# Half of an output projection moved, in bursts of four matmuls, into the attention ahead of it

## The reference, cut to what matters

```python
def dilated_mixer(x, norm_gain, w_q, q_gain, w_o, k_sh, v_sh, cos, sin):
    ...
    for g, (window, dilation) in enumerate(DIL_GROUPS):      # three groups
        o_g, lse_g = dilated_group_attention(q[:, :, g], k_sh[:, :, g], v_sh[:, :, g], window, dilation)
    ...
    wts = jax.nn.softmax(jnp.stack(lses, axis=0), axis=0)
    o = jnp.sum(wts[..., None] * jnp.stack(outs, axis=0), axis=0)
    return o.astype(x.dtype).reshape(B, S, H * D) @ w_o

def squared_relu_mlp(x, gain, w_up, w_down):
    h = rms_norm_2(x, gain)
    return jnp.square(jax.nn.relu(h @ w_up)) @ w_down

x = x + dilated_mixer(x, ...)
x = x + squared_relu_mlp(x, m_norm[layer], m_w_up[layer], m_w_down[layer])
```

## Time and profile before

| | |
|---|---|
| median of 3 runs | 2930.29 us |
| the profiled execution's own time | 2930.43 us |
| its span in the profile | 2928.6 us |
| PE busy | 2835.1 us (97%) |
| DVE busy | 1732.2 us (59%) |
| ACT busy | 1224.2 us (42%) |
| POOL busy | 1080.7 us (37%) |

### The profile page before, as it was taken

How to read it: one execution, slowest core, us unless ns; L and a number is a source line. 1 busy time by engine, 2 the same in 40 slices (tenths; PEclk the granted TensorE clock), 3 DMA queues, 4 the chain that set the end, 5 groups by cost and what they waited for, 6 DMA issues and landing times.

```text
span 2928.6 us, 39102 instructions
## 1 busy us (share of the span) xinstructions
PE 2835.1 (97%) x13391; PEld 2317.9 (79%) x13402; DVE 1732.2 (59%) x2111; ACT 1224.2 (42%) x2067; POOL 1080.7 (37%) x498
## 2 busy tenths in 40 slices
PE   6999999999899999999889999999999999999999
PEld 5767788887777888888667888888888888888887
DVE  7487776775566544658566333557566766644333
ACT  3574432223564422244454222356566665522221
POOL 1312344443213444444324444444412342244443
PEclk9999999999899999999999999999999999999999
DMA  6255263643102333332003333333301321133332
GB/s 218 87 166 194 80 207 100 202 132 100 37 29 79 93 97 96 93 94 89 29 23 95 97 96 93 94 95 89 94 22 52 95 87 30 51 94 94 100 94 93
DMA packets 366140, 278.96 MB, mean 95 GB/s; under 512 B 13618, under 2 KB 321203, under 8 KB 366003
## 3 DMA queue, kind: packets, MB, share of 16 engines
q1 hardware_dynamic: 364752, 276.83, 31.0%
q10 hardware_dynamic: 1251, 0.33, 0.0%
HBM read 275.03 MB, written 2.10 MB: 95 GB/s over the span
## 4 chain that ended last, share of the span: by engine, by line
PE 65%; issue 3%; DVE 2%; ACT 2%; POOL 1%; DMA 0%; POOLq 0%; DVEq 0%; ACTq 0%; SPq 0%
PE banks L1186 13%; PE banks L1181 12%; PE banks L1190 12%; PE banks L1050 6%; PE banks L1056 6%; PE banks L1053 6%; PE banks L1455 2%; PE banks L1023 1%; PE banks L1395 1%; PE banks L1183 1%; PE banks L1384 0%; PE banks L1091 0%; POOL w_lo L895 0%; PE banks L1428 0%; PE banks L1430 0%
## 5 line engine op out<-in xcount | busy, mean ns | idle before, releaser
L895 POOL TENSOR_TENSOR w_lo<-w_raw,w_hi 128x1024 fp32r<-128x1024 f32 (+2 forms) x431 | 1030.2, 2390 | 1692.7 <-ACT w_hi L1703 1691.6
L1703 ACT ACTIVATE w_hi<-w_raw 128x1024 fp32r<-128x1024 f32 (+2 forms) x432 | 447.2, 1035 | 1117.4 <-PE banks L1190 783.9
L1050 PE MATMUL banks<-w_hi,h_hi 128*128 128x512 f32 x960 | 386.6, 403 | 0.7 <-ACT h_hi L1884 0.7
L1056 PE MATMUL banks<-w_lo,h_hi 128*128 128x512 f32 x960 | 377.0, 393 | 0.7 <-POOL w_lo L895 0.7
L1053 PE MATMUL banks<-w_hi,h_lo 128*128 128x512 f32 x960 | 376.0, 392 | 0.7 <-DVE h_lo L601 0.7
L1181 PE MATMUL banks<-h_hi,w_hi 128*128 128x512 f32 x1280 | 339.7, 393 | 8.2 <-ACT h_hi L1884 6.3
L1186 PE MATMUL banks<-h_lo,w_hi 128*128 128x512 f32 x1280 | 321.1, 391 | 2.5 <-DVE h_lo L601 2.4
L1181 PEld LDWEIGHTS banks<-h_hi,w_hi 128*128 128x128 f32 x1280 | 241.4, 189 | 65.4 <-issue 10.6
L1186 PEld LDWEIGHTS banks<-h_lo,w_hi 128*128 128x128 f32 x1280 | 240.3, 188 | 57.8 <-DVE h_lo L601 8.6
L1190 PE MATMUL banks<-h_hi,w_lo 128*128 128x512 f32 x1152 | 284.5, 389 | 0.0
L1190 PEld LDWEIGHTS banks<-h_hi,w_lo 128*128 128x128 f32 x1152 | 216.3, 188 | 44.8
(11 more groups left out here) (373 smaller groups left out, 4252.0 us busy)
## 6 DMA issues: line engine op xcount, KB each, us to landing
Z<-in_ada_w SPq DMA_DIRECT2D x64, 512.0 KB, 5.5
w_raw<-in_m_w_up SPq DMA_DIRECT2D x64, 512.0 KB, 4.0
w_raw<-in_m_w_down SPq DMA_DIRECT2D x64, 512.0 KB, 3.7
w_raw<-in_kv_w SPq DMA_DIRECT2D x48, 512.0 KB, 3.7
w_raw<-in_ffn_w_gate SPq DMA_DIRECT2D x44, 512.0 KB, 3.7
w_raw<-in_ffn_w_up SPq DMA_DIRECT2D x44, 512.0 KB, 3.7
tmp<-in_ada_w SPq DMA_DIRECT2D x32, 512.0 KB, 4.6
w_raw<-in_ffn_w_down SPq DMA_DIRECT2D x32, 512.0 KB, 3.9
```

Of the source, the lines that this page charges most:

```text
L895: pool.tensor_tensor(wlo[j][:, 0:n], raw[j][:, 0:n], whi[j][:, 0:n], ALU.subtract).then_inc(s_wlo, 1)
L1050: pe.matmul(t, hh, wh, start=k == 0, stop=False)
L1056: mm = pe.matmul(t, hh, wl, start=False, stop=k == DC - 1)
L1703: act.activation(whi[par][:, 0:kc * P], raw[par][:, 0:kc * P], ACT.Copy).then_inc(s_whi, 1)
```

## The change

The last projection is cut in two by its inner dimension. The first four chunks (heads of pairs 0 to 3) become a stage of their own, `second_half`: eight units of 12 matmuls, which PE runs within the attention's second half, in bursts of four, in parts q = 0, 1, 2 and 4, 5, 6 of each pair (in the first pair 4, 5, 6 only); the last unit runs behind the last values. All eight accumulate in bank 7. Their weights take half of buffer 0 each (`fill_tile`), since the attention uses buffer 1. For that the maxima's groups of these pairs go round three banks, 0, 1, 2, and the wait for `diagonal` stands at group 0. ACT, POOL and DVE get the copies, splits and additions of the eight units at fixed places of their order. The stage behind the attention keeps the other four chunks, 12 matmuls a unit. ACT now copies its first unit's weights behind `inverse` of the last pair, and its second unit's behind `y_high`; before, the first stood ahead of the attention and the second in the last pair.

```diff
@@ -460,7 +460,10 @@
                 panel(a["kv_w_2"], 3 * D + g * D + half * S, 24 + 4 * g, perm=g, fold="kv_norm")
             steps.append(("dil", 4 * half))
             panels[-1].first_pair = 4 * half
-        gemm_stage("down", 8, DC, a["b_w_o_2"][0], "y", gate=None)
+        wo = a["b_w_o_2"][0]
+        second_half = Stage("down", DC, FILL, [cols_of(wo, 0, FILL, j * P, 2 * P) for j in range(2)], "y")
+        gemm_stage("down", DC, DC - FILL, wo, "y", k0=FILL * P, gate=None)
+        steps[-1][1].first_chunk = FILL
         mlp(1)
         steps.append(("bar", None))
 
@@ -476,7 +479,7 @@
             if kind == "diff":
                 st = next(st for k, st in steps[n:] if k == "gemm")
                 st.early = st.after_diff = True
-        stages = [st for k, st in steps if k in ("gemm", "diff")]
+        stages = [second_half if k == "dil" else st for k, st in steps if k in ("gemm", "diff") or (k == "dil" and st == NB)]
         for s0, s1 in zip(stages, stages[1:] + [None]):
             s0.next_kc, s0.next = s1.kc if s1 else None, s1
             assert s0.base % 2 == 0
@@ -681,9 +684,17 @@
         dil_inverse = TMP[:, 12 * VW + 2 * S:12 * VW + 3 * S]
         dil_spread = TMP[:, 12 * VW + 3 * S:12 * VW + 3 * S + 2 * P]
 
+        def dil_ring(p):
+
+            return 4 if p < NB else 3
+
         def dil_bank(p, f):
 
-            return bank[(6, 7)[f % 2] if p % NB == 0 else DIL_BANKS[f % 4]]
+            return bank[(6, 7)[f % 2] if p % NB == 0 else DIL_BANKS[f % dil_ring(p)]]
+
+        def fill_tile(t, l):
+
+            return t[0][:, l % 2 * FILL * P:(l % 2 + 1) * FILL * P]
 
         def dil_turned(p):
             return dil_bank(p, 6)[:, P:P + 2 * NB]
@@ -911,6 +922,11 @@
                 zero([dil_rows(t, 0, par, HALF[1 - par]) for par in range(2) for t in (whi[1], wlo[1])]
                      + [t[:, first:first + 8, :] for first in (8, 16, 0) for t in by_quarter])
                 pool.wait_ge(dl["scores"], past(8 * base + 4))
+                if base:
+                    for l in range(DC):
+                        u = second_half.base + l
+                        pool.wait_ge(s_whi, past(u + 1))
+                        pool.tensor_tensor(fill_tile(wlo, l), raw[l % 2][:, 0:FILL * P], fill_tile(whi, l), ALU.subtract).then_inc(s_wlo, 1)
 
             def zero(todo):
                 for rows in todo:
@@ -1077,8 +1093,8 @@
 
                 half, m, first = f % 2, dil_bank(p, f), p % NB == 0
                 g = f // 2 + 1 if f < 4 else 0
-                pe.wait_ge(dl["reduced"], past(8 * p + f - (1 if first else 3)))
-                if f == 2:
+                pe.wait_ge(dl["reduced"], past(8 * p + f - (1 if first else dil_ring(p) - 1)))
+                if f == (2 if first or p < NB else 0):
                     pe.wait_ge(dl["diagonal"], past(3 * p))
                 if f in (0, 2, 4):
                     pe.wait_ge(dl["q_high"], past(3 * p + (2 if first and g == 0 else BY_GROUP[g])))
@@ -1455,6 +1471,25 @@
                             mm = pe.matmul(o, dil_vals[:, at:at + P], dil_probs[q % 2][:, own:own + width], start=g == 0 and c == 0, stop=g == 2 and c == NB - 1, skip_group_check=True)
                     mm.then_inc(e["values_added"], 1)
 
+                def fill(l, first=0, n=3 * FILL):
+
+                    par, u = l % 2, second_half.base + l
+                    if first == 0:
+                        if l:
+                            pe.wait_ge(evac[1 - par], past((u - 1) // 2 + 1))
+                        else:
+                            pe.wait_ge(e["reduced"], past(8 * base + 8))
+                            pe.wait_ge(e["output_high"], past(FILL))
+                            pe.wait_ge(e["output"], past(2 * FILL))
+                        pe.wait_ge(s_whi, past(u + 1))
+                        pe.wait_ge(s_wlo, past(u + 1))
+                    for i in range(first, first + n):
+                        k, part = divmod(i, 3)
+                        w, y = ((whi, yhi), (wlo, yhi), (whi, ylo))[part]
+                        mm = pe.matmul(bank[7], fill_tile(w, l)[:, k * P:(k + 1) * P], ch(y, k), start=i == 0, stop=i == 3 * FILL - 1)
+                    if i == 3 * FILL - 1:
+                        mm.then_inc(gemm, 1)
+
                 last = next(st for st in panels if st.first_pair == base)
                 zero_rows_in(2)
                 for p in range(base, base + NB):
@@ -1474,7 +1509,11 @@
                             zero_rows_in(2)
                         for f in ahead.get(q, []):
                             dil_fill(p + 1, f)
+                        if base and q % 4 < 3 and (q >= 4 or p > base):
+                            fill(2 * (p - base) + q // 4 - 1, 4 * (q % 4), 4)
                     values(p, 7)
+                if base:
+                    fill(DC - 1)
 
             def diff(st):
                 e = df
@@ -2078,6 +2117,13 @@
 
                     act.activation(ch(hhi, c), ch(xT, c), ACT.Copy).then_inc(n_hi, 1)
 
+                def fill_high(l):
+
+                    u = second_half.base + l
+                    act.wait_ge(w_raw[u % 2], 16 * (u // 2 + 1))
+                    act.wait_ge(gemm, past(u - 1))
+                    act.activation(fill_tile(whi, l), raw[u % 2][:, 0:FILL * P], ACT.Copy).then_inc(s_whi, 1)
+
                 last = next(st for st in panels if st.first_pair == base)
                 following = last.next
                 act.wait_ge(gemm, past(last.base + last.n))
@@ -2090,6 +2136,8 @@
                     probs(p, 0)
                     if old is not None:
                         take(p - 1, 1)
+                    if base:
+                        fill_high(max(2 * (p - base), 1))
                     if new is not None:
                         for par in range(2):
                             q_high(new, 1, par)
@@ -2122,8 +2170,10 @@
                     if new is not None:
                         q_high(new, 0, 0)
                         q_high(new, 0, 1)
-                    else:
+                    elif base == 0:
                         high(following.kc, 1, following.base + 1, following.base // 2, following, 1)
+                    if base and p > base:
+                        fill_high(2 * (p - base) + 1)
                     probs(p, 5)
                     if old is not None:
                         y_high(p - 1)
@@ -2140,10 +2190,14 @@
                 take(p, 0)
                 take(p, 1)
                 inverse(p)
+                if base:
+                    high(following.next.kc, 0, following.next.base, following.next.base // 2)
                 if base == 0:
                     h_again(6)
                     h_again(7)
                 y_high(p)
+                if base:
+                    high(following.next.kc, 1, following.next.base + 1, following.next.base // 2)
 
             def diff(st):
                 e = df
@@ -2790,16 +2844,28 @@
                     negate(p)
                     class_spread(p)
 
+                def take_fill(l):
+
+                    if not base:
+                        return
+                    u = second_half.base + l
+                    dve.wait_ge(gemm, past(u + 1))
+                    dve.tensor_tensor(ch(xT, l), bank[7], ch(xT, l), ALU.add).then_inc(evac[u % 2], 1)
+
                 def prepare(new, old):
 
                     if new is not None:
                         k_low(new, 1)
                     if old is not None:
                         output(old - 1)
+                        if new is None:
+                            take_fill(5)
                     if new is not None:
                         reduce(new, 0)
                         k_low(new, 2)
                         reduce(new, 1)
+                        if old is not None:
+                            take_fill(2 * (old - base) - 1)
                         reduce(new, 2)
                         reduce(new, 3)
                         rows_spread(new)
@@ -2830,6 +2896,7 @@
                         class_spread(p)
                     q_low(p, 2)
                     prepare(p + 1 if p < base + NB - 1 else None, p if p > base else None)
+                    take_fill(2 * (p - base))
                 p, h_lows = base + NB - 1, iter(DIL_LOWS)
                 again = next(n for n in norm_list if n.raw and not n.fresh)
 
@@ -2843,6 +2910,7 @@
                     low_again(6)
                     low_again(8)
                 output(p)
+                take_fill(DC - 1)
                 sub_low(p)
                 if base == 0:
                     dve.wait_ge(e["output"], past(2 * p + 2))
```

## The result

The changed kernel took 2934.74 us (median of 12 runs, 2930.84 to 2939.85), the kernel before 2930.13 us in the same rounds (12 runs, 2927.48 to 2933.70): ratio 1.0016, 95% interval 1.0008 to 1.0023. By the ratio that is 4.7 us slower (2.3 to 6.7). The forecast was 6.6 us slower, 2936.9 us in a range of 2933.0 to 2940.5. The growth of 0.16% is inside what I had called "no change" (0.2%), to which I had given less (0.39) than to a time beyond it (0.57).

A forecast was written before the change was run, and what follows sets the result against it. PE, busy 97% of the span, was taken as the bound, with little waiting to fill. The terms +1.0 - 1.5 + 2.45 + 3.86 + 0.8 gave +6.6 us on 2930.3: 2936.9 us, 8-in-10 range 2933 to 2940.5.

The forecast's parts named there:

- Part 1: Pairs 4 to 7 and projection: 96 matmuls leave (-21.8 us), return as bursts (19.05) and a last unit (2.72); net zero.
- 6: The seven other projection units behind the attention: 84 matmuls in 19.05 us without a gap, saving counted in Part 1.
- Part 2: Entry of bursts in the pairs: 12 of 21 cost 0.085 us each, +1.0 us (bounds 0 and 1.8).
- Part 3: Pairs 5 and 6: the two PE waits of 0.76 us for ACT go, -1.5 us (bounds -1.5 and 0).
- Part 4: Pairs 4 to 7: additions free bank 7 with 0.61 us of room, and three maxima banks suffice; cost 0.
- rival B: Bank 7's handover in the pairs comes late as POOL's splits delay DVE: +4.0 us, 2940.9 us; chance 0.12.
- Part 5: Behind the last value matmuls (end T): PE idles 2.7 us for late-split weights, unit done at T+8.34, +2.45 us (0 to 3).
- Part 7: Projection's end to the MLP's second unit: waits for weights and DVE, 9.75 us instead of 5.89, +3.86 us (1.0 to 5.5).
- model stage: The differential attention's projection, same code and sizes, taken as pattern: 9.75 us from its end to the MLP's second unit.
- Part 8: Behind the tail's wait: the clock may fall to half for 3.3 us; +0.8 us taken (bounds 0 and 1.65).
- rival A: Tail and MLP entry: new waits smaller than modelled, about no change, +2.9 us, 2933.2 us; chance 0.17.
- C: Value matmuls in the pairs: bursts overlap about 7.6 us of waiting for weights, sum -2.0 us, 2928.3 us; chance 0.06.

The follow-up runs named there:

- ring-only kernel: Kernel before, with three banks instead of four for the score matmuls from pair 4 on and no projection work moved; ratio 0.9999 to the kernel before.
- late bursts: Changed kernel with the same 84 matmuls in 14 bursts of six behind tiles 2, 3, 6 and 7; ratio 1.0026 to the kernel before.
- early copy: Changed kernel with ACT's weight copy for the remaining stage's first unit ahead of the last pair's takes and inverse; ratio 1.0012 to the kernel before.
- seven bursts: Changed kernel with the 84 matmuls in 7 bursts of 12 behind tiles 0 and 4; ratio 1.0032 to the kernel before.
- woven kernel: Changed kernel with the bursts of tiles 5 and 6 woven into the value matmuls ahead of them; ratio 1.0033 to the kernel before.
- addition first: Changed kernel with DVE's last addition ahead of the previous unit's low part and square sum, in both half stages; ratio 1.0007 to the kernel before.

## Why the prediction was right, and where it was off

The mechanism was the forecast one and not a rival's; sign and size held. Of the signs that I had named, pairs 5 and 6 (26.20 us each), 4 (23.37) and 7 (21.37), the tail's wait and the projection's 19.05 came as written; the whole stretch came to 133.8 us instead of about 135.5, and no low clock stood behind either wait.

- **Part 1, moved work, and 6.** Right. Removed and added matmuls cancel, the seven units take 19.05 us.
- **Part 2, entry of a burst.** Over-sized. Laid beside the ring-only kernel start by start, the 21 bursts cost 0.71 us beyond 84 x 0.2268, instead of 1.0: 0.07 to 0.08 each behind 128-column maxima matmuls, 0.01 to 0.03 behind all others. Bursts of two and of six gave 0.03 each. My price was a misreading of the earlier trace rows: the projection's second matmul does come 0.31 us after its first, but the first comes only 0.03 us after the last value matmul (2520.86), not 0.11, so the two steps together hold an entry of 0.01 us. That 1.0 is near 0.71 is partly luck. The Trainium skill ("TensorE: Matmul & The Clock Gate", "Step-by-step: what each phase is for") says that weight loads are pulled ahead of running matmuls; an entry of nothing, which the prediction took from that, is nearer to most of these places than my 0.085.
- **Part 3, the waits for ACT.** The mechanism is right: the 1.2 us of idle time is gone, and it returns in the kernel with late bursts. The size was too small. Against the ring-only kernel each wait gives back 0.89 us, 0.78 at its end and 0.10 since the next matmul behind a wait comes after 0.32 us instead of 0.22: 1.8 us and not 1.5.
- **Part 4, bank 7 and the ring.** Right: pairs of 79.10 us with either ring, room 0.63 us against 0.61 worked out. Two kernels show what the room hangs on. The collision that rival B needs did not occur: in the pairs all seven additions take 0.68 to 0.69 us, and in pairs 5 to 7 the splits start 2.8 to 4.1 us after an addition.
- **Part 5, tail.** Right: unit done at T + 8.31 against T + 8.34 worked out. The cause, ACT's order, is shown by the early copy.
- **Part 7, MLP entry.** 3.37 us instead of 3.86. The model stage contained a stretch of half clock, this execution doesn't; in seven executions of other kernels that have the old order of DVE and no such stretch, the model stage takes 9.28 to 9.58 us, so the stretch is worth 0.2 to 0.5 of its 9.75. I had noted that DVE's delay hides most of that stretch, and yet left the rest of it in this term.
- **Part 8, clock.** +0.8 taken, 0 in this profile. Over all kernels: PE stood for 2.31 to 2.49 us in the tail of five, and the clock fell to 0.50 behind three of them (about 1.6 us lost each: with seven bursts, 9.79 + 19.14 against 8.31 + 19.05). So half of it was a fair price for the mean of many runs, and no single profile can show it.

The pairs grew by 97.14 - 78.98 = 18.16 us for 19.05 us of moved work, so parts 2 and 3 are -0.9 together instead of -0.5. The sum by the profile is -0.89 + 2.42 + 3.37 = +4.9 us. With the clock's share (3 of 5 times 1.6, an estimate of +1.0) it would be 5.9; the timed runs say 4.7 (2.3 to 6.7), which holds both.

The measured +4.7 lies between rival A (+2.9) and the forecast, but both new waits came nearly in full, which is not A's mechanism. C is refuted by the woven kernel and by the 256-column value instructions: the 0.110 us hold no waiting for weights that other matmuls could fill. Why no time was gained is settled too: there was 1.2 us of waiting in the pairs to fill, and halving the units behind cost 5.8.

## What to carry to other kernels

Before work is moved out of a stage to fill gaps, count the gaps, and then ask what the longer stage was hiding: here 24-matmul units covered a weight ring, a queue order and DVE's tail, and 12-matmul units did not, while 18-matmul units covered the ring and DVE's tail (the queue order was mended there by the early copy). Where one accumulation bank is handed round, its margin is made of what stands between the last reduction and the next use; write that number down and apply it to every later edit. Effects of 1 to 2 us in 2930 are read from stretches cut at the same instructions, not from the median, and a price is read from the step ahead of an instruction as well as from the one behind it.

## What the hardware showed that I had not expected

- Executions with the same order of work up to there differ by 8.4 us in where pair 4 begins (2437.95 to 2446.33), at mean granted clocks of 0.990 to 0.994.
- The fall to half clock behind a wait is a matter of chance near these lengths: behind 18 waits of 1.71 to 2.01 us at these two MLP entries it came twice, behind seven waits of 2.29 to 2.49 us five times. The two without it are the 2.47 us of the kernel after and the 2.48 us with the addition first; nor did it come behind the 2.24 us of the earlier trace rows.
- A 128-column value instruction takes 0.110 us and a 256-column one 0.216 (two of each in 0.65 us, 2475.85 to 2476.50 in the kernel after): 0.11 us for each 128 columns, where the projection's matmuls take 0.2268 / 4 = 0.057. The half rate is no idle time, and a 512-column matmul in between hides none of it.
